# ScalarE's order in layer 0's attention: both exponentials of a tile ahead of the first copy

## The chip, the core and the metric

The kernel runs on one core of one Trainium2 chip. A core has five engines, each with its own instruction stream, that meet through semaphores: TensorE (matrix products and transposes, results into PSUM), VectorE, ScalarE, GpSimd and SyncE, which starts DMA transfers. The metric is the device time of one execution in microseconds (us), the median of the runs. A profile is one execution, in which every instruction's start and duration is recorded; its span runs from the first to the last instruction of the program.

## What is computed

A two-layer diffusion backbone over 1024 latent tokens and 256 context tokens, width 1024, all in fp32. Layer 0 mixes tokens by a pooling mixer beside differential attention; layer 1 by latent attention; each layer ends with a SwiGLU block. The change touches the differential attention of layer 0 alone:

```python
def diff_attn_core(q, k, v, lam, scale):
    s = jnp.einsum('bqhjd,bkhjd->bhjqk', q.astype(F32), k.astype(F32)) * scale
    p = jax.nn.softmax(s, axis=-1)
    pd = p[:, :, 0] - lam * p[:, :, 1]
    return jnp.einsum('bhqk,bkhe->bqhe', pd, v.astype(F32)).astype(v.dtype)
```

There are 4 heads, each with two score maps (j = 0, 1) of head width 64, and values of width 128. Latent queries see all 1280 keys; context queries see the 256 context keys. The output of each head is normalised (rmsnorm over its 128 values) afterwards.

## The kernel before

`attention0` (line 175) is one block of five engine programs. It works on N = 40 score tiles: tile n is head n // 10 and query tile q = n % 10 of 128 queries. Tiles with q < 8 are latent queries (full tiles, 1280 keys), q = 8 and 9 are context queries (256 keys). Two neighbouring tiles form a pair J (20 pairs), whose combined probabilities are transposed ("turned") in units of two key blocks: five units a pair, one for the context pair. `("u", x)` is the turn of a unit, `("v", x)` its product with the values. The order is written out by hand, in periods n:

- TensorE, in period n: the latent scores of the first map (`latent(t, 0)`, line 316; they wait for the first exponential of the tile before), then the turns of list `a`, the context scores of tile n (`context(n)`, line 306; they wait for both exponentials of tile n - 1), the latent scores of the second map (`latent(t, 1)`), then turns (line 341) and value products (line 355) of list `b` in turn, then extras.
- `work_in(n)` gives the lists. In odd n, with J = (n - 3) / 2: `a` is the turn of unit 4 of pair J - 1; `b` is value 3 of J - 1, turn 0 of J, value 4 of J - 1, turn 1 of J. In even n, with J = (n - 4) / 2: `a` is turn 2 of J; `b` is value 0, turn 3, value 1, value 2 of J. Units that a pair doesn't have drop out.
- `extras_in(n)`: in tiles 17, 27 and 37 the sums of squares of the head before (`s`, line 365, 10 products with one column), in tiles 19 to 23, 29 to 33 and 39 to 41 its factors (`b`, line 371, two transposes). They too write one of the two turn banks in PSUM.
- The turn banks: `tbank` deals them out alternately in the order of all turns and extras, and `bank_free` makes each wait until the one two back has been read: for a turn that is ScalarE's copy.
- VectorE takes the maximum over the latent scores (line 465) and context scores (line 472; 474 in context tiles), then the negated maximum of the two for each map (`negative`, line 479), the bias of the exponential. After E0 can start it computes the factor of the tile before (lines 485, 489), and then the maximum over the second map's latent scores, and that map's negated maximum. In the first tile of heads 1 to 3 both negated maxima come together, since those scores were made during the head before.
- ScalarE takes the exponentials with their row sums (`exps(n, 0)` and `exps(n, 1)`, line 413), the copies of turned units from PSUM to `pt` (`copy`, line 423), of outputs (`copy_out`, line 430), a square root for each head (line 456) and the high part of normed outputs (line 435). `exps(n, 1)` waits for `comb` (the tile two back is combined) and, in full tiles, for the second negated maximum.
- GpSimd scales the second map by its factor and adds it to the first (`combine`, lines 553, 556, 557). Turn 0 of a pair waits until both its tiles are combined.

ScalarE's loop before, lines 437 to 451 (the two statements that change places are in the middle):

```python
for n in range(PERIODS):
    a, b = work_in(n)
    ...
    if n < N:
        exps(n, 0)
    for x in turns_of(b)[:1]:
        copy(x)
    if n < N:
        exps(n, 1)
    for J in outs_of(b):
        copy_out(J)
    for x in turns_of(b)[1:]:
        copy(x)
```

The copy in the middle is that of turn 0 of a pair in odd tiles and of turn 3 in even tiles; 19 odd tiles and 15 even tiles below 40 have one.

Of the kernel before, what the change touches and what calls it, by code (L numbers as in the profile page):

```python
# [174 lines left out]
def attention0(e, qs, ks, vs, P, p1, pt, o_sb, sq, tmp, ahi, alo, pooled, mixp, w_out):  # L175
# [3 lines left out]
    N, PT, RING_P = 10 * HEADS0, 6, 6  # L179
    PAIR_COUNT, PERIODS = 5 * HEADS0, 10 * HEADS0 + 12  # L180
    first_unit = [sum(len(PAIRS0[y % 5]) for y in range(J)) for J in range(PAIR_COUNT + 1)]
    with ExitStack() as ctx:
# [10 lines left out]
        def latents_before(n):  # L193

            return 8 * (n // 10) + min(n % 10, 8)
# [17 lines left out]
        def work_in(n):  # L213

            if n % 2:
                J = (n - 3) // 2
                a = [("u", unit(J - 1, 4))]
                b = [("v", unit(J - 1, 3)), ("u", unit(J, 0)), ("v", unit(J - 1, 4)), ("u", unit(J, 1))]
            else:
                J = (n - 4) // 2  # L220
                a = [("u", unit(J, 2))] + [("v", unit(J, 0))] * (J == PAIR_COUNT - 1)
                b = [("v", unit(J, 0))] * (J < PAIR_COUNT - 1) + [("u", unit(J, 3)), ("v", unit(J, 1)), ("v", unit(J, 2))]
            return [[x for x in y if x[1] is not None] for y in (a, b)]
# [4 lines left out]
        def extras_in(n):  # L228

            return ([("s", h) for h in range(HEADS0) if SUMS_AT[h] == n]  # L230
                    + [("b", h, p) for h in range(HEADS0) for p in range(5) if SCALES_AT[h][p] == n])

        def turns_of(work):
            return [x for x in work if x[0] == "u"]

        def outs_of(work):
            return [pair_of(x[1])[0] for x in work if x[0] == "v" and x[1] + 1 == first_unit[pair_of(x[1])[0] + 1]]
# [4 lines left out]
        def last_turn(n):  # L242

            return turn_index["u", first_unit[n // 2 + 1] - 1]

        def tbank(x):
            return TB + turn_index[x] % 2 * BANK
# [4 lines left out]
        with nc.Block() as block:  # L252
            @block.sync
            def _(sp):
                def values(h):
                    if h >= 2:
                        sp.wait_ge(s["pv"], 21 * (h - 1))
                    sp.dma_start(vs[:, h % 2, :, :].rearrange("p t v -> p (t v)"), S["v0"][h, :, :]).then_inc(s[f"v{h % 2}"], 16)

                values(0)  # L260
                e.store_turn(sp, 19)
                for i in range(8, 12):
                    e.store_u(sp, i)
                for x, n in e.turns_stored:
                    sp.wait_ge(x, n)
                for h in range(1, HEADS0):
                    if h >= 2:
                        sp.wait_ge(s["ctx"], 10 * (h - 1))
                    load_keys0(e, sp, ks[h % 2], h, s[f"qk{h % 2}"])
                    load_queries0(e, sp, qs[h % 2], h, s[f"qk{h % 2}"])  # L270
                    values(h)
                for y in range(4):
                    sp.wait_ge(e.ustored[y], 48)
                sp.wait_ge(s["ctx"], N)
                u, pw, edge = pooled
                for g in range(3):
                    load_pooled(e, sp, u, g)
                    if g == 0:
                        sp.dma_start(edge[:], e.dram["pool_edge"]).then_inc(e.pool_edge, 16)
                        sp.dma_start(pw[:], e.dram["pool_w"]).then_inc(e.pool_w, 16)  # L280
                for x in range(RING):
                    load_block(e, sp, mixp, 0, x, w_out[x, :, :])
                e.clear_old(sp)

            @block.tensor
            def _(pe):
# [72 lines left out]
                def extra(x):  # L359
                    bank_free(x)  # L360
                    if x[0] == "s":
                        h = x[1]
                        pe.wait_ge(s["sq"], 5 * h + 5)
                        for q in range(10):
                            last = nc.tensor.matmul(e.ps[:, tbank(x) + q:tbank(x) + q + 1], sq[:, h % 2, q * 128:(q + 1) * 128], e.sel[:, 2:3],
                                                    start=True, stop=True)
                    else:
                        _, h, p = x
                        pe.wait_ge(s["rd"], h + 1)
                        for y, q in enumerate(tiles(h, p)):  # L370
                            last = nc.tensor.transpose(e.ps[:, tbank(x) + y * 128:tbank(x) + (y + 1) * 128],
                                                       rd[:, q:q + 1].broadcast_to([128, 128]), e.ident[:])
                    last.then_inc(s["turn"], 1)
# [21 lines left out]
            @block.scalar  # L395
            def _(act):
                def exps(n, m):
                    h, q = divmod(n, 10)
                    a = 0 if q < 8 else LAT
                    if m == 0:  # L400
                        if n >= RING_P:
                            act.wait_ge(s["turn"], last_turn(n - RING_P) + 1)
                        act.wait_ge(s["n0"], n + 1)
                        src, dst = e.ps[:, M0 + a:M0 + T], P[:, n % RING_P, a:T]
                        total = s0[:, h % 2, q:q + 1]
                    else:
                        if n >= 2:
                            act.wait_ge(s["comb"], n - 1)
                        if q < 8:
                            act.wait_ge(s["n1"], latents_before(n) + 1)  # L410
                        src, dst = e.ps[:, M1 - CTX:M1 + LAT - a], p1[n % 2][:, 0:T - a]
                        total = s1[:, n % 2:n % 2 + 1]
                    nc.scalar.activation(dst, src, ACT.Exp, bias=nb[:, n % 4, m:m + 1], accum_out=total).then_inc(s[f"e{m}"], 1)

                def copy(x):
                    u = x[1]
                    if u == 0:
                        for y in range(4):
                            act.wait_ge(e.ustored[y], 48)
                    act.wait_ge(s["turn"], turn_index[x] + 1)  # L420
                    if u >= PT:
                        act.wait_ge(s["pv"], u - PT + 1)
                    nc.scalar.activation(pt[:, u % PT, :], e.ps[:, tbank(x):tbank(x) + BANK], ACT.Copy).then_inc(s["copy"], 1)

                def copy_out(J):
                    h, p = divmod(J, 5)
                    act.wait_ge(s["pv"], first_unit[J + 1])
                    if h >= 2:
                        act.wait_ge(s["tmp"], 5 * (h - 2) + p + 1)
                    nc.scalar.activation(o_sb[:, h % 2, 256 * p:256 * p + 256], e.ps[:, OB:OB + 256], ACT.Copy).then_inc(s["out"], 1)  # L430

                def normed(h, p):
                    x = 5 * h + p
                    act.wait_ge(s["tmp"], x + 1)
                    nc.scalar.activation(ahi[:, h, 256 * p:256 * p + 256], tmp[:, x % 2, :], ACT.Copy).then_inc(s["nhi"], 1)

                for n in range(PERIODS):
                    a, b = work_in(n)
                    for x in turns_of(a):
                        copy(x)  # L440
                    for J in outs_of(a):
                        copy_out(J)
                    if n < N:
                        exps(n, 0)
                    for x in turns_of(b)[:1]:
                        copy(x)
                    if n < N:
                        exps(n, 1)
                    for J in outs_of(b):
                        copy_out(J)  # L450
                    for x in turns_of(b)[1:]:
                        copy(x)
                    for x in extras_in(n - 1):
                        if x[0] == "s":
                            act.wait_ge(s["vv"], x[1] + 1)
                            nc.scalar.activation(sd[:], vv[:], ACT.Sqrt).then_inc(s["sd"], 1)
                    for x in extras_in(n):
                        if x[0] == "b":
                            normed(*x[1:3])
# [4487 lines left out]
```

## Time and profile before

| | |
|---|---|
| time, median of 3 runs | 3234.47 us (3230.9 to 3235.47) |
| the profiled execution's span | 3233.6 us |
| TensorE busy (PE) | 3044.6 us, 94% |
| TensorE weight loads (PEld) | 2491.6 us, 77% |
| GpSimd busy (POOL) | 2288.7 us, 71% |
| VectorE busy (DVE) | 1947.3 us, 60% |
| ScalarE busy (ACT) | 1105.4 us, 34% |
| layer 0's attention | from about 302 to 549 us of the span |

Engines are named as in the profile: PE is TensorE's products, PEld its weight loads, which overlap with them, DVE VectorE, ACT ScalarE, POOL GpSimd. A row of the timeline has the start in us from the span's start, the duration in us from the first of the merged instructions to the end of the last, engine, line, operation, output<-inputs by tile names, output shape<-input shape and the number of merged instructions. In square brackets stands how long the engine had been idle before it, and who ended that; no bracket means that the engine came straight from other work. Tiles in PSUM are all called `ps`. The two buffers of the second exponential are `squares` in even tiles and `a_p` in odd ones; the first exponential always writes `a_p`.

### The profile page before, as it was taken

Reading aid. Unit: us, or ns where it says so; the run is one execution under the profiler, and the core shown is the slowest. Engines: PE = TensorE matmul, PEld = TensorE weight load, DVE = VectorE, ACT = ScalarE, POOL = GpSimd, SP = SyncE. Lnnn points to the kernel's source line nnn. Section 1 sums busy time; section 2 is a strip of 40 time slices with the busy share of each in tenths; the row PEclk is TensorE's granted clock in tenths of the full one; section 3 lists DMA queues with packets and bytes.
Section 4 is the critical chain, followed back from the end, with each engine's and each line's share of the span. In section 5 each row is a group of like instructions: output and inputs, shape, how many; then the busy total and the mean of one; then the engine's idle time right before and its main releaser. Section 6 shows DMA issues by size and latency. Waiting matters only on the chain. (4 is left out here: it accounts for less than half of the span.)

```text
span 3233.6 us, 44078 instructions
## 1 busy us (share of the span) xinstructions
PE 3044.6 (94%) x14302; PEld 2491.6 (77%) x14302; DVE 1947.3 (60%) x2544; ACT 1105.4 (34%) x1897; POOL 2288.7 (71%) x2297
## 2 busy tenths in 40 slices
PE   7998998998989999999898989999998999999999
PEld 6777876787968888888676767777776778888887
DVE  6585665777864454454535557777765765454454
ACT  4322775134620110010333446766772410010110
POOL 4584765663498888888623268888887688888885
PEclk9999998999999999999998979999999999999999
DMA  6367323457621111112203441111114211111112
GB/s 237 110 203 202 75 58 117 174 170 262 217 79 59 45 52 60 52 43 65 102 26 105 149 130 41 48 41 40 48 29 141 68 40 58 45 52 58 51 46 85
DMA packets 134922, 297.72 MB, mean 92 GB/s; under 512 B 36449, under 2 KB 69473, under 8 KB 134689
## 3 DMA queue, kind: packets, MB, share of 16 engines
q1 hardware_dynamic: 121632, 252.89, 24.8%
q10 hardware_dynamic: 13184, 43.52, 4.3%
q8 instruction: 55, 0.90, 0.1%
q14 instruction: 51, 0.41, 0.0%
HBM read 251.68 MB, written 44.63 MB: 92 GB/s over the span
## 5 line engine op out<-in xcount | busy, mean ns | idle before, releaser
L1546 POOL TENSOR_TENSOR a_pl<-a_p,a_ph 128x512 fp32r<-128x512 f32 x320 | 451.1, 1430 | 102.9 <-ACT a_p L1491 98.1
L164 PE MATMUL ps<-a_q,a_k 97*128 97x512 f32 x960 | 273.3, 398 | 1.3 <-POOL a_q L1565 1.3
L1490 ACT ACTIVATE a_ph<-ps 128x512 fp32r<-128x512 f32 x320 | 192.2, 601 | 179.4 <-PE ps L164 178.6
L1392 DVE TENSOR_REDUCE a_top<-ps 128x1 f32<-128x512 f32 x256 | 172.3, 687 | 95.4 <-PE ps L1316 95.4
L164 PE MATMUL ps<-hidden,whi 128*128 128x512 f32 x704 | 218.0, 391 | 7.2 <-POOL wlo L1849 4.3
L164 PE MATMUL ps<-mixed_hi,l_whi 128*128 128x512 f32 (+1 forms) x544 | 207.2, 381 | 10.3 <-issue 2.9
L3032 POOL TENSOR_TENSOR l_wlo<-l_raw,l_whi 128x512 fp32r<-128x512 f32 x154 | 200.4, 1301 | 12.8
L164 PEld LDWEIGHTS ps<-a_q,a_k 97*128 97x128 f32 x960 | 179.8, 191 | 38.2 <-issue 1.5
L164 PE MATMUL ps<-mixed_lo,l_whi 128*128 128x512 f32 (+1 forms) x544 | 206.4, 379 | 0.0
L164 PE MATMUL ps<-mixed_hi,l_wlo 128*128 128x512 f32 (+1 forms) x544 | 206.2, 379 | 0.0
L2485 DVE SCALAR_TENSOR_TENSOR residual<-ps,mod,residual 128x512 f32<-128x512 f32 x176 | 132.1, 750 | 109.8 <-PE ps L164 109.8
L3832 DVE SCALAR_TENSOR_TENSOR residual<-ps,mod,residual 128x512 f32<-128x512 f32 x176 | 132.0, 750 | 108.5 <-PE ps L164 108.5
L1849 POOL TENSOR_TENSOR wlo<-raw,whi 128x512 fp32r<-128x512 f32 x144 | 187.8, 1304 | 12.0
L1491 ACT ACTIVATE a_p<-ps 128x512 f32<-128x512 f32 x320 | 192.7, 602 | 0.0
L3236 PE MATMUL ps<-l_factor,l_whi 128*128 128x512 f32 x528 | 164.1, 392 | 7.2 <-POOL l_wlo L3032 7.2
L164 PEld LDWEIGHTS ps<-hidden,whi 128*128 128x128 f32 x704 | 132.7, 189 | 35.7 <-issue 8.0
L1584 PE MATMUL ps<-mixed_hi,l_whi 128*128 128x256 f32 (+1 forms) x472 | 147.8, 313 | 10.8 <-POOL mixed_lo L3106 3.3
L2054 PE MATMUL ps<-l_factor,whi 128*128 128x512 f32 x480 | 147.9, 389 | 0.0
L1584 PE MATMUL ps<-mixed_lo,l_whi 128*128 128x256 f32 (+1 forms) x472 | 146.6, 311 | 0.0
L1584 PE MATMUL ps<-mixed_hi,l_wlo 128*128 128x256 f32 (+1 forms) x472 | 146.3, 310 | 0.0
L3236 PE MATMUL ps<-mixed_hi,l_whi 128*128 128x512 f32 x352 | 138.0, 392 | 4.6 <-POOL l_wlo L3032 3.8
L164 PE MATMUL ps<-hidden,wlo 128*128 128x512 f32 x352 | 137.7, 391 | 0.0
(421 smaller groups left out, 8886.3 us busy)
## 6 DMA issues: line engine op xcount, KB each, us to landing
l_raw<-in_w_ffn SPq DMA_DIRECT2D x132, 512.0 KB, 3.9
raw<-in_w_ffn SPq DMA_DIRECT2D x66, 512.0 KB, 3.6
l_row<-in_mod_t ACTq DMA_DIRECT2D x32, 512.0 KB, 4.5
f_vraw<-in_mod_t ACTq DMA_DIRECT2D x24, 512.0 KB, 4.1
a_k<-scratch_k SPq DMA_DIRECT2D x32, 320.0 KB, 6.8
f_raw<-in_w_in SPq DMA_DIRECT2D x16, 512.0 KB, 5.4
l_raw<-in_w_out SPq DMA_DIRECT2D x16, 512.0 KB, 5.2
l_shared_row<-in_mod_t ACTq DMA_DIRECT2D x16, 512.0 KB, 6.3
```

The source lines that it names most:

```text
L164: last = nc.tensor.matmul(out, a, b, start=at == 0, stop=at == n - 1)
L1392: nc.vector.tensor_reduce(top[:, q:q + 1, c], e.ps[:, bank:bank + BANK], AX.X, ALU.max).then_inc(s["auxr"], 1)
L1490: nc.scalar.activation(ph[:, kk % 2, c], b, ACT.Exp).then_inc(s["exp"], 1)
L1491: nc.scalar.activation(p[:, kk % 2, c], b, ACT.Exp).then_inc(s["exp"], 1)
L1546: nc.gpsimd.tensor_tensor(pl[:, kk % 2, c], p[:, kk % 2, c], ph[:, kk % 2, c].bitcast(F32), ALU.subtract).then_inc(s["pl"], 1)
L1584: last = nc.tensor.matmul(out, a, b, start=k == 0 and x == 0, stop=k == n - 1 and x == 2)
L1849: nc.gpsimd.tensor_tensor(wl[:, slot(pos), :], of, wh[:, slot(pos), :].bitcast(F32), ALU.subtract).then_inc(s["half"], 1)
L2054: last = nc.tensor.matmul(e.ps[:, bank:bank + BANK], a[:, slot(pos), w], b, start=k == 0 and x == 0, stop=k == 3 and x == 2)
L2485: last = nc.vector.scalar_tensor_tensor(h[:, m, a:a + w], e.ps[:, o:o + w], e.mod[:, g, c:c + 1], h[:, m, a:a + w], ALU.mult, ALU.add)
L3032: nc.gpsimd.tensor_tensor(wl[:, slot(pos), :], of, wh[:, slot(pos), :].bitcast(F32), ALU.subtract).then_inc(s["half"], 1)
L3236: last = nc.tensor.matmul(e.ps[:, at:at + BANK], a[:, slot(pos), w], b, start=k == 0 and x == 0, stop=k == 3 and x == 2)
L3832: nc.vector.scalar_tensor_tensor(h[:, m, a:a + w], e.ps[:, o:o + w], e.mod[:, 40 + m, 0:1], h[:, m, a:a + w], ALU.mult, ALU.add).then_inc( ...
```

## The change

In every period in which a tile is scored, ScalarE now takes both exponentials in a row, and the copy of the first turned unit of list `b` comes behind them. The copies of list `a` stay ahead of the first exponential, the output copy and the remaining copies stay behind, and no other engine's program changes. No instruction, wait or buffer is added or removed.

```diff
@@ -442,10 +442,9 @@
                         copy_out(J)
                     if n < N:
                         exps(n, 0)
+                        exps(n, 1)
                     for x in turns_of(b)[:1]:
                         copy(x)
-                    if n < N:
-                        exps(n, 1)
                     for J in outs_of(b):
                         copy_out(J)
                     for x in turns_of(b)[1:]:
```

## Rows read from the trace of the kernel before

**Rows 1.** The page: busy us, share of the span, instructions, for each engine

```profile
PE 3044.6 (94%) x14302; PEld 2491.6 (77%) x14302; DVE 1947.3 (60%) x2544; ACT 1105.4 (34%) x1897; POOL 2288.7 (71%) x2297
```

**Rows 2.** Busy table: length, busy PE, PEld, DVE, ACT, POOL, granted clock, DMA, GB/s

```profile
302.50:537.50 235.00, 213.83 (x1178) 176.76 (x1178) 143.06 (x291) 158.79 (x288) 161.80 (x126) 0.96 0.33 86
...
458.50:462.00 3.50, 3.50 (x15) 3.10 (x15) 2.02 (x4) 0.60 (x1) 0.72 (x2) 0.59 0.00 0
```

**Rows 3.** Waits, 302 to 538 us: us in total, times, longest

```profile
ACT a_p L413 <- DVE a_negmax L479: 43.8, 33, 5.7
...
PEld ps L306 <- issue: 11.1, 13, 1.4
```

**Rows 4.** Timeline, tile 25 and the head of tile 26

```profile
443.17 1.33 ACT L413 ACTIVATE a_p<-ps,a_negmax 128x1280 f32<-128x1280 f32 x1 [1.14 <-DVE a_negmax L479]
...
444.49 0.59 ACT L423 ACTIVATE a_pt<-ps 128x512 f32<-128x512 f32 x1
...
444.67 0.15 DVE L479 TENSOR_REDUCE a_negmax<-a_max 128x1 f32<-128x2 f32 x1
...
444.97 1.33 ACT L413 ACTIVATE a_p<-ps,a_negmax 128x1280 f32<-128x1280 f32 x1
...
445.15 1.17 PE L316 MATMUL ps<-a_k,a_q 128*128 128x512 f32 x4
...
446.16 0.60 PE L341 MATMUL ps<-ident,a_p 128*128 128x128 f32 x4
...
446.27 0.40 ACT L430 ACTIVATE a_o<-ps 128x256 f32<-128x256 f32 x1
...
446.54 0.71 PE L306 MATMUL ps<-a_k,a_q 128*128 128x256 f32 x4
...
447.50 0.68 DVE L472 TENSOR_REDUCE a_max<-ps 128x2 f32<-128x512 f32 x1
```

**Rows 5.** Timeline, tile 12, which has no copy between its exponentials

```profile
370.27 1.33 ACT L413 ACTIVATE a_p<-ps,a_negmax 128x1280 f32<-128x1280 f32 x1 [1.66 <-DVE a_negmax L479]
...
372.01 1.33 ACT L413 ACTIVATE squares<-ps,a_negmax 128x1280 f32<-128x1280 f32 x1 [0.33 <-DVE a_negmax L479]
```

**Rows 6.** Timeline, tile 13's first exponential and tile 14's context scores

```profile
375.38 1.33 ACT L413 ACTIVATE a_p<-ps,a_negmax 128x1280 f32<-128x1280 f32 x1 [1.67 <-DVE a_negmax L479]
...
378.74 0.71 PE L306 MATMUL ps<-a_k,a_q 128*128 128x256 f32 x4 [0.26 <-ACT a_p L413]
```

**Rows 7.** Timeline, tile 17: first exponential and the sums of squares

```profile
397.71 1.33 ACT L413 ACTIVATE a_p<-ps,a_negmax 128x1280 f32<-128x1280 f32 x1 [1.14 <-DVE a_negmax L479]
...
399.77 2.29 PE L365 MATMUL ps<-sel,a_sq 128*128 128x1 f32 x20
```

**Rows 8.** Timeline, tile 23 and the head of tile 24

```profile
431.19 1.33 ACT L413 ACTIVATE a_p<-ps,a_negmax 128x1280 f32<-128x1280 f32 x1 [1.36 <-DVE a_negmax L479]
...
432.51 0.59 ACT L423 ACTIVATE a_pt<-ps 128x512 f32<-128x512 f32 x1
...
433.15 0.43 PE L371 MATMUL ps<-ident,a_rstd 128*128 128x128 f32 x2 [0.95 <-ACT a_pt L423]
...
433.34 1.17 PE L316 MATMUL ps<-a_k,a_q 128*128 128x512 f32 x4
...
434.95 0.66 PE L341 MATMUL ps<-ident,a_p 128*128 128x128 f32 x4 [0.44 <-ACT a_pt L423]
...
435.36 0.61 PE L306 MATMUL ps<-a_k,a_q 128*128 128x256 f32 x3
```

**Rows 9.** Timeline, tile 20's first exponential and tile 21's first turn

```profile
415.56 1.33 ACT L413 ACTIVATE a_p<-ps,a_negmax 128x1280 f32<-128x1280 f32 x1 [0.93 <-DVE a_negmax L479]
...
418.49 0.60 PE L341 MATMUL ps<-ident,a_p 128*128 128x128 f32 x4
```

**Rows 10.** Timeline, tile 11's context scores

```profile
363.29 0.53 PEld L306 LDWEIGHTS ps<-a_k,a_q 128*128 128x128 f32 x4 [0.28 <-issue]
```

**Rows 11.** Timeline, tile 9's first turn in list b

```profile
356.00 0.42 PEld L341 LDWEIGHTS ps<-ident,a_p 128*128 128x128 f32 x4 [0.66 <-POOL a_p L557]
```

## Prediction

> **What bounds the kernel now.** I read the page first: TensorE is busy 94% [rows 1] of a span of 3233.6 us, and the weight products of the later stages, which the change doesn't touch, follow in the same order. So the question is what happens to the end of layer 0's attention. The busy table of that stage [rows 2] covers 235.0 us: TensorE is busy 213.8 of them, ScalarE 158.8, GpSimd 161.8, VectorE 143.1. The reader is to see two things there: ScalarE has a third of its time free, so its total work sets nothing, and TensorE has only 21 us free. The table of waits of the stage [rows 3] says for whom ScalarE waits: 43.8 us in 33 waits for VectorE's negated maximum (line 479), the bias of an exponential. Last, the timeline of one full tile, number 25 [rows 4], for the order and the distances.
>
> In tile 25 the first exponential (below: E0) starts at 443.17, the copy of the first turned block at 444.49, the second exponential (E1) at 444.97. VectorE finishes the second map's negated maximum at 444.67 + 0.15 = 444.82, so E1 starts only 0.15 after its bias is there, 1.80 after E0. Meanwhile TensorE goes from the next tile's scores (445.15) to the turn (446.16) and the context scores (446.54) without an idle stretch. That turn writes the PSUM bank that the copy of 444.49 empties: there are two banks, and bank_free makes each turn wait for the copy two turns back.
>
> **What moves.** No instruction is added or removed. 34 tiles have such a copy (19 odd, 15 even); each now stands behind E1.
>
> *What E1 gains.* Next to nothing in a full tile: where no copy stands between, tile 12, E0 starts at 370.27 and E1 at 372.01, 1.74 later, after a wait of 0.33 for line 479 [rows 5]. With the copy it is 1.80. The other bound is 1.32 (444.49 - 443.17), the distance to an instruction that waits for nothing, a gain of 0.48. I take 0.06: in tile 25 the maximum is ready 1.65 after E0, which fits a start at 1.74.
>
> *What the copy loses.* E1 now starts at E0 + 1.74; what follows E1 without a wait starts 1.30 behind it (444.97 to 446.27), so the copy starts at E0 + 3.04 instead of E0 + 1.32 and ends, 0.59 long, at E0 + 3.63: 1.72 later. Whether that costs anything is decided by who wants the bank, tile by tile. A turn that waited starts 0.06 after the copy's end (I take this from tile 23, where the factor's 433.15 follows a copy of 0.59 that began 1.32 behind E0, at 432.51), and the context scores follow 0.41 behind it (434.95 to 435.36) [rows 8]; queued it is 0.38 (446.16 to 446.54). So a waiting turn comes at E0 + 3.69, the context scores at E0 + 4.10.
>
> 1. Tiles 5, 15, 25, 35: the turn at the head of the next tile wants the bank. Tile 25: context scores at 443.17 + 4.10 = 447.27 instead of 446.54: +0.73, on an engine with no idle stretch here. 4 x 0.73 = 2.9.
> 2. Tiles 3 and 13: same turn. TensorE waited for E1 anyway, context scores at 378.74 [rows 6]; they come at 375.38 + 4.10 = 379.48: +0.74. 1.5.
> 3. Tile 7: the same 0.73, but in tile 9 TensorE stands 0.66 for GpSimd [rows 11], whose chain follows the context maximum. In the like tile VectorE starts that maximum at 447.50, 0.25 after the context scores' end (446.54 + 0.71) [rows 4], and absorbs as much. +0.5.
> 4. Tiles 17, 27, 37: the sums of squares (line 365) take the bank at the end of the same tile, ahead of the next scores. Tile 17: 397.71 + 3.69 = 401.40 instead of 399.77 [rows 7]: 1.63, and VectorE and GpSimd hang behind it alike. 3 x 1.6 = 4.8.
> 5. Tiles 23 and 33: the factor (line 371) takes it. It waited already, at 433.15; now 431.19 + 3.69 = 434.88, +1.73, and the scores behind it 433.34 + 1.73 = 435.07. The turn after them had waited until 434.95 and now comes 1.01 behind the scores (445.15 to 446.16), 436.08, the context scores at 436.46 instead of 435.36 [rows 8]: +1.1. 2.2.
> 6. Tiles 20 and 30, even, with a factor in them: the turn at the head of the next tile wants the bank. In the first tile of a head VectorE makes both negated maxima together, so E1 can start at E0 + 1.32, the copy at + 2.62, its end at + 3.21: 415.56 + 3.27 = 418.83 instead of 418.49 [rows 9], 0.3, and 0.4 at the context scores. 0.8.
> 7. Tile 10, the same without a factor: the bank isn't wanted, E1 comes up to 0.48 sooner, and TensorE stood 0.28 for it [rows 10]: -0.3.
> 8. The other even full tiles (4, 6, 14, 16, 24, 26, 34, 36): the bank and the late block are wanted only in the second half of the next tile: 0. Tiles 11, 21, 31: no turn follows; E1's 0.06 each, -0.2. The eight context tiles (exponentials of 256 columns): the first copy there waits for TensorE, not for its place; their E1 comes sooner, which can help by 0 to 0.48 at the three boundaries where a square root follows. Nearest is tile 9, where TensorE waits for GpSimd [rows 11], so -0.1 each, -0.3.
>
> Sum: 2.9 + 1.5 + 0.5 + 4.8 + 2.2 + 0.8 - 0.3 - 0.2 - 0.3 = **+11.9 us**. The cover of the even tiles in group 8 is the distance between a turn and its product; were it gone, each would cost some 0.73 as in group 1, 5.8 for the eight. Behind the stage everything starts later by the same amount; its first weight blocks are asked for when the last context scores are done, and shift along.
>
> One rule bears on a term. ScalarE frees itself 1.32 after an exponential's start by the row. The Trainium skill (ScalarE: Activation LUTs, What ACT_TABLE_LOAD costs) says that activations back to back overlap by about 93 ns; by it the distance would be 1.24, and the sum some 1 us smaller. The row decides.
>
> **Rivals.** *A: TensorE steps around the wait.* The scores behind a waiting factor have their own semaphore met; if TensorE ran them ahead, the stalls would shrink to almost nothing: 3234.5. Against it: at 433.15 the factor waited for a copy though the scores behind it had been free since E0's end at 431.19 + 1.33 = 432.52, and they started at 433.34, behind it [rows 8]. The Trainium skill (TensorE: Matmul & The Clock Gate, Architectural detail) gives TensorE's queue a partial reorder window that pulls weight loads ahead of matmuls in flight; of going past a wait it claims nothing. 0.06.
>
> *B: faster.* If the second maximum were ready at E0 + 1.32, E1 would come 0.48 sooner, and the context scores, ahead of which the weight loads stand idle 13 times (11.1 us, line 306; the table says issue, the product side names ScalarE [rows 3, 6]), with it: 13 x 0.48 = 6.2, and with 0.3 for the square roots 6.5, provided no bank is wanted: 3228. It decides from the point where line 479 ends before the copy starts; in tile 25 it ended 0.33 after that, and the 33 waits speak against it. 0.03.
>
> *C: the clock falls more.* From 458.5 to 462.0, right behind the sums of squares of the second head, the granted clock was 0.59 [rows 2], between the levels 2.4 and 1.2 GHz: (1 - 0.59) x 3.5 = 1.4 us of work pushed back. New stalls stand just ahead of the three blocks of sums. Three more such stretches give +4.2: 3250.6. If the stretches of before vanish, about -2.8. The Trainium skill (same page, Part 1) has the gate throttled by default and released by activity, which agrees in direction; the rows don't show where the point lies. 0.13.
>
> *D: something else holds those turns anyway* (GpSimd's combined tile): 3234.5. Against it, the timeline names the copy in tile 23, and in tile 25 nothing. 0.04.
>
> **Numbers.** The forecast, 0.74: the profiled run's span 3233.6 + 11.9 = 3245.5; the median of the runs is 0.9 above that span, so 3246.4. Ends: releases 0.2 cheaper in 11 places and stretches of low clock that vanish give -5; rival C gives +4.2, and the runs of before spread from 3230.9 to 3235.5, so I add 2. Range 3240.5 to 3252.5, which leaves out A, B and D (0.13) and some of C. 0.2% is about 6.5 us, what a measurement of this kernel can tell from no change. Faster 0.03; same A, D and the forecast halved: 0.12; slower 0.85.
>
> **What would show it.** In the changed profile: E1 1.74 behind E0 in full tiles, the copy 3.04 behind E0; idle time of TensorE on line 341 for ScalarE's copy up to about 7 us, on line 365 three new waits of 1.6; the context scores of tiles 24 and 34 late by 1.1; ScalarE's busy time unchanged; the stage longer by about 12 and nothing behind it longer. Wrong if line 306 rather than 341 carries the new idle time, if E1 comes at 1.32, or if a copy's delay is felt in the even tiles of group 8.

## The result and the profile after

The changed kernel takes 3254.44 us (median of 4 runs, 3249.99 to 3258.06) against 3233.08 us for the kernel before, measured beside it: a ratio of 1.0058, interval 1.0043 to 1.0072. A second measurement, below, gave 1.0063 (1.0049 to 1.0078). By these ratios it is slower by 19 to 20 us (by the two differences of medians 21 and 23), where 12 were forecast; the median lies 1.9 us above the upper end of the range.

The page of the changed kernel; the profiled execution is the slowest of the four:

```profile
span 3256.3 us, 44078 instructions
...
PE 3057.2 (94%) x14302; PEld 2501.1 (77%) x14302; DVE 1950.5 (60%) x2544; ACT 1109.8 (34%) x1897; POOL 2287.6 (70%) x2297
```

ScalarE's busy time is nearly that of before, 1109.8 us for 1105.4. The busy table cuts the run at the context scores of tile 3, those of tile 39 (the "stage" from here on) and the last factor. Before first; the columns are those of [rows 2]:

```profile
321.85:522.78 200.93, 188.44 (x1069) 158.50 (x1069) 127.00 (x259) 141.00 (x255) 147.88 (x113) 0.98 0.23 55
522.78:546.18 23.40, 16.75 (x101) 13.35 (x100) 8.05 (x20) 11.95 (x27) 12.61 (x19) 0.89 0.47 166
546.18:3233.60 2687.42, 2556.56 (x11848) 2084.95 (x11848) 1610.18 (x1974) 847.92 (x1445) 1944.52 (x2053) 0.98 0.26 83
```

The changed kernel, cut at the same places:

```profile
320.14:542.02 221.88, 197.69 (x1068) 165.03 (x1069) 128.74 (x259) 145.35 (x255) 147.80 (x113) 0.95 0.21 50
542.02:565.38 23.36, 16.89 (x101) 13.42 (x99) 8.12 (x20) 11.71 (x27) 12.74 (x19) 0.89 0.47 166
565.38:3256.30 2690.92, 2562.28 (x11848) 2089.53 (x11848) 1611.50 (x1974) 848.14 (x1445) 1943.20 (x2053) 0.97 0.26 83
```

The stage is 221.88 us instead of 200.93, +20.95; the end of the attention is as long as it was; the 2690 us behind it are 3.5 us longer. In the 13 other profiles of this document, of kernels that are all alike there, that last stretch lay between 3.2 us shorter and 5.4 us longer than in the first profile of before: it is no effect of the change, but it hides small ones in the time.

Two things stand in the stage. The first is the waits. Tile 25 and the head of tile 26, as in [rows 4]; line numbers behind the edit are one lower than before:

```profile
451.28 1.33 ACT L413 ACTIVATE a_p<-ps,a_negmax 128x1280 f32<-128x1280 f32 x1 [1.14 <-DVE a_negmax L478]
...
452.78 0.15 DVE L478 TENSOR_REDUCE a_negmax<-a_max 128x1 f32<-128x2 f32 x1
...
453.02 1.33 ACT L413 ACTIVATE a_p<-ps,a_negmax 128x1280 f32<-128x1280 f32 x1 [0.32 <-DVE a_negmax L478]
...
454.34 0.59 ACT L423 ACTIVATE a_pt<-ps 128x512 f32<-128x512 f32 x1
...
454.98 0.66 PE L341 MATMUL ps<-ident,a_p 128*128 128x128 f32 x4 [0.54 <-ACT a_pt L423]
...
455.40 0.72 PE L306 MATMUL ps<-a_k,a_q 128*128 128x256 f32 x4
...
456.15 0.69 DVE L471 TENSOR_REDUCE a_max<-ps 128x2 f32<-128x512 f32 x1 [0.45 <-PE ps L306]
```

E1 stands 1.74 behind E0 after a wait of 0.32 for VectorE's negated maximum, as tile 12 did before [rows 5]; the copy starts 3.06 behind E0 instead of 1.32; TensorE's turn waits 0.54 for it (its weight load 0.98), and VectorE, which had come straight from its latent maximum, now waits 0.45 for the context scores. Tile 17 [rows 7]:

```profile
399.53 1.33 ACT L413 ACTIVATE a_p<-ps,a_negmax 128x1280 f32<-128x1280 f32 x1 [1.15 <-DVE a_negmax L478]
...
402.58 0.59 ACT L423 ACTIVATE a_pt<-ps 128x512 f32<-128x512 f32 x1
...
403.23 2.39 PE L365 MATMUL ps<-sel,a_sq 128*128 128x1 f32 x20 [1.47 <-ACT a_pt L423]
```

The sums start 3.70 behind E0, where 3.69 was forecast, after 1.47 of idle time. At the factor of tile 23 TensorE already stood 0.95 before [rows 8]; now it stands 2.69:

```profile
440.32 0.43 PE L371 MATMUL ps<-ident,a_rstd 128*128 128x128 f32 x2 [2.69 <-ACT a_pt L423]
```

The waits of the stage with the changed order ([rows 3] is the same view of before):

```profile
ACT a_p L413 <- DVE a_negmax L478: 47.3, 48, 5.9
...
PEld ps L341 <- ACT a_pt L423: 10.8, 12, 1.5
...
PEld ps L306 <- issue: 10.4, 10, 1.6
...
PEld ps L371 <- ACT a_pt L423: 9.5, 5, 2.9
...
PEld ps L365 <- ACT a_pt L423: 5.1, 3, 1.7
```

Before, line 341's loads stood 4.8 us for the copy, line 371's 4.4, line 365's nothing. ScalarE's waits for the maximum went from 33 to 48: some of them had been hidden by the copy that stood in front.

The second thing is TensorE's clock. Five stretches of the changed kernel; their granted clock is the third number from the end:

```profile
406.50:410.00 3.50, 3.50 (x14) 3.11 (x13) 2.26 (x4) 1.42 (x5) 0.44 (x1) 0.51 0.00 0
440.60:444.20 3.60, 3.60 (x15) 3.10 (x14) 1.75 (x3) 1.17 (x3) 1.79 (x3) 0.53 0.00 0
467.90:474.90 7.00, 7.00 (x28) 6.31 (x28) 2.40 (x6) 0.68 (x2) 0.18 (x1) 0.51 0.00 0
505.50:509.00 3.50, 3.39 (x12) 2.89 (x13) 1.44 (x2) 1.07 (x4) 2.17 (x3) 0.51 0.00 0
532.80:539.70 6.90, 6.90 (x30) 6.43 (x31) 1.71 (x6) 1.70 (x6) 1.23 (x2) 0.51 0.02 4
```

Before had only the like of the third and the last, and those half as long:

```profile
459.10:462.50 3.40, 3.40 (x13) 2.90 (x12) 2.15 (x4) 0.60 (x1) 0.12 (x1) 0.50 0.00 0
517.10:520.60 3.50, 3.50 (x16) 3.02 (x14) 1.94 (x6) 1.16 (x3) 1.31 (x2) 0.51 0.03 7
```

All are at 1.2 GHz. By the clock records of the trace the stage spends 23.9 us at that level, before 6.8. The first, third and last begin within 4 us of the start of the sums of squares of tiles 17, 27 and 37, the other two at the factors of tiles 23 and 33.

### The profile page after: what moved, and what is told of

The parts are those of the page before. It is cut to its first block and busy times, and to the rows that moved or that the text cites. A ratio compares the mean times of both kernels' runs of the same rounds, so it can differ in the third digit from the quotient of the medians.

```text
span 3256.3 us, 44078 instructions
## 1 busy us (share of the span) xinstructions
PE 3057.2 (94%) x14302; PEld 2501.1 (77%) x14302; DVE 1950.5 (60%) x2544; ACT 1109.8 (34%) x1897; POOL 2287.6 (70%) x2297
```

## The experiments

Each compares its stage, from the context scores of tile 3 to those of tile 39, with 197.64 us, the length that the kernel before has with no half-clock time in it (experiment 7). "Waits" is the time by which the stage grows through later context scores alone, tile by tile. Where the clock was low in a tile, the step is taken from a run that had the full clock there (4, 8 and 9); those of 3, 5 and 6 are in part estimates of this kind.

The recorded expectations reckon with 12.7 us for the changed kernel. It is 13.1: they count each block of sums with the 1.64 by which it starts later, but the context scores behind it come 1.73 to 1.74 later at full clock, since a block that had to wait takes 2.39 us instead of 2.30. "Theory 1" in them is the reading just given: only a turn, factor or block of sums that wants the bank of the late copy stalls TensorE, and the long ones of these stalls bring the clock down too.

| kernel | stage | waits | at half clock | time, ratio to before |
|---|---|---|---|---|
| before, first and second profile | 200.93, 200.91 | 0 | 6.8, 6.8 | 1 |
| changed | 221.88 | 13.1 | 23.9 | 1.0058 (1.0043 to 1.0072) |
| changed, again | 223.39 | 13.1 | 27.3 | 1.0063 (1.0049 to 1.0078) |
| 1 even tiles alone | 202.94 | 0.5 | 10.2 | 0.9994 (0.9985 to 1.0004) |
| 2 turn tiles alone | 204.56 | 5.3 | 3.4 | 1.0004 (0.9995 to 1.0014) |
| 3 sum and factor tiles alone | 214.32 | 7.4 | 20.5 | 1.0056 (1.0040 to 1.0073) |
| 4 changed, stalls filled | 215.46 | 13.1 | 10.2 | 1.0042 (1.0028 to 1.0055) |
| 5 before, TensorE waits longer | 217.36 | 8.5 | 23.9 | 1.0058 (1.0038 to 1.0078) |
| 6 changed, sums and factors later | 215.40 | 11.4 | 13.7 | 1.0056 (1.0037 to 1.0074) |
| 7 before, wide sums | 197.64 | 0 | 0 | 0.9986 (0.9975 to 0.9997) |
| 8 changed, wide sums | 215.50 | 13.1 | 10.2 | 1.0039 (1.0024 to 1.0054) |
| 9 changed, filled and wide | 212.32 | 13.1 | 3.4 | 1.0031 (1.0020 to 1.0042) |
| 10 wide sums, both in a row in tile 10 and context tiles | 197.51 | 0 | 0 | 0.9986 (0.9975 to 0.9997) |

In every row with low clock the stage is 197.6, plus the waits, plus 0.45 to 0.48 us for each us at half clock: some 1.6 us for a stretch of 3.4.

**Which copies cost: 1 to 3.** The changed order in some tiles alone; `both` is the one thing that differs:

```diff
+                    both = n % 2 == 0                        # 1, even_tiles
+                    both = n in (3, 5, 7, 13, 15, 25, 35)    # 2, turn_tiles
+                    both = n in (17, 23, 27, 33, 37)         # 3, extra_tiles
                     if n < N:
                         exps(n, 0)
+                    if n < N and both:
+                        exps(n, 1)
                     for x in turns_of(b)[:1]:
                         copy(x)
-                    if n < N:
+                    if n < N and not both:
                         exps(n, 1)
```

> Both exponentials in a row in the even tiles alone (15 of the 34 moved copies). Theory 1 (only a turn or factor that wants the bank of the late copy stalls TensorE): stalls of 0.3 to 0.4 in tiles 20 and 30, tile 10 gains 0.3, nothing elsewhere; the context scores of tile 39, counted from those of tile 3, are at most 0.5 us later than before, and the time is that of before within 1 us. Theory 2 (every moved copy costs alike, 20.9 us of the stage over 34 copies = 0.6 each): 15 x 0.6 = 9 us later.

> Both in a row only in tiles 3, 5, 7, 13, 15, 25 and 35, where a turn at the head of the next tile wants the bank. Theory 1: 0.75 each, 0.5 in tile 7: the stage is 5.0 us longer, and no new stretch of low clock appears in it, since the stalls are short: time 5 us above before. If short stalls bring the clock down too: new half-clock stretches behind these tiles, 1.7 us each, and 7 us or more.

> Both in a row only in tiles 17, 23, 27, 33 and 37, where the sums of squares or a factor want the bank. The waits alone: 3 x 1.64 + 2 x 1.1 = 7.1 us. Theory 1 (the long stalls ahead of these also bring the clock down, as in the changed kernel's trace at 406, 440, 468, 505 and 533 us): 7 + about 8 = 15 us, with five or so low stretches. Rival (the low stretches come from where the clock's phase happens to lie, not from these stalls): 7 us, and low stretches as in before.

The waits came as theory 1 had them. Even tiles: 0.32 in tiles 20 and 30, -0.31 in tile 10, nothing in the eight of group 8; theory 2 falls. The stage was nevertheless 2.0 us longer, because the clock fell once more than before, behind the sums of tile 17, where nothing had been made to wait (busy table of even tiles alone):

```profile
401.00:404.60 3.60, 3.60 (x15) 3.17 (x14) 2.41 (x5) 1.62 (x5) 0.69 (x1) 0.53 0.00 0
```

Turn tiles: 0.80, 0.77, 0.75, -0.21 (given back in front of tile 10), and 0.75 four times, and less half-clock time than before rather than more: the clock fell behind the sums of tile 27 alone. Its time, 1.3 us above before (-1.6 to 4.5), doesn't resolve the 3.6 us of its stage. Sum and factor tiles: the sums 1.64 later three times, the context scores behind the factors 1.1 twice, and 20.5 us at half clock, in these stretches of the busy table of that kernel:

```profile
402.40:406.00 3.60, 3.60 (x14) 3.10 (x13) 2.26 (x4) 1.16 (x3) 0.22 (x1) 0.53 0.00 0
436.50:440.20 3.70, 3.70 (x15) 3.17 (x14) 2.05 (x3) 1.07 (x3) 1.67 (x3) 0.54 0.00 0
463.80:467.40 3.60, 3.60 (x15) 3.11 (x16) 1.19 (x3) 0.00 (x0) 0.00 (x0) 0.53 0.00 0
498.00:504.90 6.90, 6.14 (x20) 5.17 (x21) 3.23 (x7) 3.16 (x7) 3.33 (x4) 0.51 0.01 2
528.80:532.30 3.50, 3.50 (x14) 2.94 (x13) 1.37 (x4) 1.41 (x4) 1.61 (x2) 0.52 0.01 2
```

By the stage these five tiles of 34 bring 13.4 of the 20.95 us: 7.4 of waits and the rest clock. By the time (1.0056) it looks like the whole loss, but the interval reaches down to 1.0040, and the profiled execution, 3243.4 us, is the fastest of four that otherwise took 3254 to 3256.

**Does the order matter, or the stall: 5.** ScalarE's order is that of before:

```diff
+                    if n in (17, 23, 27, 33, 37):
+                        pe.wait_ge(s["copy"], work_in(n)[1][-1][1] + 1)
                     for x in extras_in(n):
                         extra(x)
```

> The kernel before, ScalarE's order untouched; in tiles 17, 23, 27, 33 and 37 TensorE waits, ahead of the sums of squares or the factor, until the copy of turn 1 is done too (it ends at 401.69 in tile 17 of before, 434.90 in tile 23). Theory 1 (a stall of TensorE there costs its length and brings low clock, whoever makes it): 3 x 1.98 at the sums and 2 x 1.2 at the context scores behind the factor, 8.3 us of waits, and about 6 of clock: 14 us, as the kernel with both exponentials in a row in these tiles. Rival (the order on ScalarE itself costs something, as later maxima or factors): 8 us at most and the clock as before.

The sums came 1.97 later three times and the clock spent 23.9 us at half. The stage is 16.4 us longer than before, 8.5 of waits and 8 of clock, more than the 14 expected and less than the changed kernel's 20.95, which has the waits of the turn tiles too; the ratio 1.0058 (1.0038 to 1.0078) doesn't resolve that difference. Its timeline at tile 17, the last exponential and the block of sums:

```profile
398.00 1.33 ACT L415 ACTIVATE a_p<-ps,a_negmax 128x1280 f32<-128x1280 f32 x1
...
400.23 2.39 PE L365 MATMUL ps<-sel,a_sq 128*128 128x1 f32 x20 [1.80 <-ACT a_pt L425]
```

So a stall of TensorE there has this price, with ScalarE's order as before: the stall costs, and not the order itself.

**Filling the stall: 4.** Real products in it, the order and every wait of the changed kernel kept:

```diff
+                    if n in (17, 23, 27, 33):
+                        if n % 10 == 7:
+                            arrived((n + 3) // 10)
+                        latent(scores_in(n + 1), 0, True)    # no semaphore; overwritten
                     for x in extras_in(n):
                         extra(x)
```

> The changed kernel, and in tiles 17, 23, 27 and 33 TensorE makes the first map's scores of the next tile once more, ahead of the sums of squares or the factor: 1.2 us of real products that lie inside the stall of 1.6 or 1.7 and are overwritten. Nothing is left out. Theory 1: the waits stay what they are, the low stretches at 406, 440, 468 and 505 go, that at 533 (tile 37, not filled) stays: 12 + 2 = 14 us above before, 6 to 7 below the changed kernel. Rival (low stretches by phase alone): as the changed kernel, 21 us above before, or more by the work added.

The timeline of tile 17, products of the filling and the sums behind them:

```profile
401.65 0.85 PE L316 MATMUL ps<-a_k,a_q 128*128 128x512 f32 x3
...
403.04 2.39 PE L366 MATMUL ps<-sel,a_sq 128*128 128x1 f32 x20 [0.54 <-ACT a_pt L428]
```

And of tile 23, the filling and the factor:

```profile
437.89 1.20 PE L316 MATMUL ps<-a_k,a_q 128*128 128x512 f32 x4 [0.45 <-ACT a_p L418]
...
440.12 0.43 PE L372 MATMUL ps<-ident,a_rstd 128*128 128x128 f32 x2 [1.03 <-ACT a_pt L428]
```

The sums still wait for the copy (0.54, the rest is now work) and come 1.64 late; the factor's 2.69 of idle time is now 0.45, products, and 1.03. At the two factors the low stretches are gone: the context scores of tiles 24 and 34 come 1.09 and 1.10 later, the forecast's 1.1, where the changed kernel had 2.1 and 2.4. Behind the sums of tiles 17 and 27 they stayed, against the expectation. The one of tile 27 is half as long, but so is that of tile 37, which was not filled, so that this can't be put down to the filling. A stall of 0.54 is left there; that a fall needs none is shown by before and by the even tiles alone.

**The sums themselves: 7 and 8.**

```diff
-    nc.tensor.matmul(e.ps[:, tbank(x) + q:tbank(x) + q + 1], sq[...], e.sel[:, 2:3], ...)
+    nc.tensor.matmul(e.ps[:, tbank(x) + 48 * q:tbank(x) + 48 * q + 48], sq[...], e.sel[:, 2:50], ...)
```

VectorE's read of the sums is changed with it, to take the first of each 48.

> The kernel before; the sums of squares are made with 48 columns of ones instead of one (all 48 results alike, VectorE reads the first), so that TensorE streams columns while it loads the squares as weights. Theory 1's second half says that the low clock behind tiles 27 and 37 of before (459 and 517 us) comes from the block of one-column products itself: no stretch of low clock between 310 and 540 us, the block's own length unchanged (0.115 a product), the stage 3 us shorter, time 0.1% lower. Rival (the stretches are chance): low stretches as before, or the block longer.

> The changed kernel with the same 48 columns in the sums. Waits as in the changed kernel, 12.7 us. Theory 1: the low stretches behind the sums (406, 468 and 533 us there, 17 us at half clock together) go or shorten, those at the factors (440, 505) stay, 6.8 us: stage 12.7 + 0.46 x 0 to 7 us, 13 to 16 us longer than before. If the stalls ahead of the sums bring the clock down and not the sums: as the changed kernel, 20 us.

In the kernel before, no half-clock time is left in the stage, and the block is as long as with one column (2.33 us; 2.29 in tile 17 of before [rows 7]). A block of sums in the timeline of that kernel:

```profile
454.81 2.33 PE L365 MATMUL ps<-sel,a_sq 128*128 128x48 f32 x20
```

The stage in its busy table:

```profile
320.30:517.94 197.64, 185.38 (x1068) 155.84 (x1069) 127.00 (x259) 140.94 (x255) 146.62 (x113) 1.00 0.23 56
```

The stage is 3.3 us shorter and the time 0.14% lower (0.03 to 0.25). With the changed order the stretches behind tiles 17 and 37 went; one behind tile 27 stayed, 6.8 us long, and one at the factor of tile 33. That at the factor of tile 23 went too, against the expectation and though TensorE stood 2.69 there as before. Where a stall of 1.5 stands ahead, wide sums don't always help. Which of the two decides in a given place stays open.

**Both remedies: 9.**

> The changed kernel with both remedies: the next scores made once more inside the stalls of tiles 17, 23, 27 and 33, and 48 columns in the sums of squares. It separates waits from clock. Theory 1: every wait as in the changed kernel, the granted clock 1.00 or one stretch at most (tile 37), so that the stage (context scores of tile 3 to those of tile 39) is 197.6, as before with wide sums, + 12.7 = 210.3 us. If the waits had been sized wrongly and the clock counted for less, the length stays near 215.

The stage in the busy table of this kernel:

```profile
320.46:532.78 212.32, 192.77 (x1085) 159.38 (x1085) 126.78 (x259) 145.22 (x255) 146.89 (x113) 0.99 0.22 53
```

212.3 with one stretch of 3.4 us left, in tile 37, which was not filled: 197.6 + 13.1 + 1.6. The expectation, 210.3 and one stretch at most, was short by 0.4 in the waits. With the clock nearly taken out, the waits are 1.2 above the forecast's 11.9.

**If TensorE went around the wait: 6.** The extras of tile n stand behind `latent(t, 0)` of period n + 1.

> The changed kernel with TensorE's sums of squares and factors issued behind the next tile's first scores instead of ahead of them (the order of the turn banks stays). What rival A asked of the hardware is here done by the program. Theory 1: in tiles 17 and 27 1.2 of the 1.64 us is covered by those scores, in 23 and 33 0.65 of the 1.1; 3.7 us less waiting, the 0.75 of tiles 3 to 35 stays: about 9 us of waits in the stage instead of 12.7. If VectorE, which takes the sums ahead of its next maximum, hands the delay on instead, the context scores of tile 19 come as late as in the changed kernel.

Half a success. In tiles 17 and 27 the next scores covered 0.9 of the 1.73 by which the context scores come later, in 23 and 33 some 0.3 of the 1.1, and the context scores of tiles 22 and 23 (32 and 33) together lost 0.4 more than with the changed order; the factors come 0.9 to 2.4 later there. Waits 11.4 instead of 13.1, where 9 was expected. That VectorE, which takes sums and factors in its own order, hands the rest on fits this and is not shown by a run of its own. The time doesn't show the shorter stage: 1.0056 (1.0037 to 1.0074), and the profiled execution is the fastest of its four.

**Better than both: 10.** Wide sums, and `both = n % 10 >= 8 or n == 10`.

> Towards a version better than both: the kernel before with wide sums, and both exponentials in a row only where the changed trace showed a gain or nothing (tile 10 and the context tiles, q = 8 and 9). Theory 1: tile 10 gives 0.3, the others 0 to 0.1 each: the stage 0.3 to 0.7 us shorter than with wide sums alone, the time 0.1 to 0.2% below before. If the order cost something by itself: longer than with wide sums alone.

Tile 11's context scores come 0.31 sooner, and tile 12's have lost 0.23 of it again. The stage is 0.13 us shorter than with wide sums alone, where 0.3 to 0.7 was expected; the ratio is the same 0.9986. The gain is that of the wide sums.

**Repeats.**

> The kernel before once more, unchanged, for a second profile of it. If the low stretches behind the sums of squares depend on where the execution stands when it reaches them, their number between 310 and 540 us differs from the two of the first profile (0 to 3), and the stage is 197.6 us + some 1.6 for each; the order of events and all waits are the same to 0.05 us. If they are fixed: two again, 200.9 us.

> The changed kernel once more, unchanged, for a second profile and a narrower interval. Theory 1: the waits of the stage as in the first profile to 0.05 us (0.75, 1.64 and so on, 12.7 in all); the low stretches behind the three blocks of sums and the two factors are there again, 17 to 24 us at half clock, since each has its cause in the program, so that the stage is 218 to 222 us and the time 17 to 21 us above before. If the stretches of the first profile were an accident of that execution: 3 to 7 us at half clock, stage 212 to 214, time 10 to 13 above before.

Before: the same two stretches, the stage the same to 0.02 us; the rival "where the execution stands" falls for these two profiles, which doesn't make the number fixed: the turn tiles alone had one such stretch and the even tiles alone three, with nothing waiting ahead of any block of sums. Changed: every wait again within 0.03, and 27.3 us at half clock instead of 23.9 (the one behind tile 17 was twice as long), which is outside what was expected, on the far side. How long a stretch gets does vary: the eight of 6.8 us at sums all began 0.7 to 1.7 us after the block's first product, inside the block, those of 3.4 us 1.8 us or more after it.

**All 14 profiles together.** Whether the clock fell, at the three blocks of sums (tiles 17, 27, 37) and the two factors (23, 33):

| place | TensorE idle just ahead | runs | falls |
|---|---|---|---|
| sums, one column | none | before twice, 1, 2 | 8 of 12 |
| sums, one column | 0.5 to 0.6 us | 4, 6 (17 and 27) | 4 of 4 |
| sums, one column | 1.5 to 1.8 us | changed twice, 3, 5; 4, 6 (37) | 14 of 14 |
| sums, 48 columns | none | 7, 10 | 0 of 6 |
| sums, 48 columns | 0.6 us | 9 (17 and 27) | 0 of 2 |
| sums, 48 columns | 1.5 us | 8; 9 (37) | 2 of 4 |
| factor | 0.9 to 1.0 us | before twice, 1, 2, 7, 10 | 0 of 12 |
| factor | 1.0 us | 4, 6, 9 | 1 of 6 |
| factor | 2.7 us | changed twice, 3, 5, 8 | 9 of 10 |

A stall makes a fall much likelier in both places, and one-column sums bring falls by themselves. What settles a single place is not shown.

## Why the forecast fell short

**The exponentials' distance: right.** 1.74 from tile 6 on in all full tiles but the first of a head, 1.32 there; tiles 2 to 5 kept 1.80. The reason named, that E1 waits for the maximum in VectorE's order, is what the new wait of 0.32 in tile 25 shows.

**The groups: right, to 0.3 us each, for groups 1 to 6.** Turn at the head of the next tile: 0.75 (0.73 forecast), 0.78 (0.74) for tiles 3 and 13, 0.53 for tile 7 (0.5), the missing part absorbed in front of tile 10 as argued. Sums: 1.64 later (1.6), the context scores behind them 1.73, a step that the forecast took to be the same. Factors of tiles 23 and 33: 1.09 at full clock (1.1). Tiles 20 and 30: 0.32 (0.4). The eight even tiles of group 8: 0. All waits together 13.1; 11.9 forecast.

**Group 7 and the small gains of group 8: wrong in size.** Tile 10's 0.31 was there, but tile 11's first exponential hangs on VectorE, which takes the latent scores first and so had no use for context scores that came sooner; 0.17 was given back a tile later. Nothing was gained at the square roots. Some 0.6 us too hopeful.

**The clock: the step that failed.** The sum has no term for it. It stood beside the sum, as rival C, with a chance of 0.13 and 1.4 us for each of three more stretches. Three more came, behind the sums of tile 17 and at both factors, and the two of before were twice as long: 17.1 us more at half clock, which cost the stage 7.9 us (20.95 - 13.1), not 4.2. The forecast's waits alone would have been 1.2 us short. The row that could have warned was one of [rows 2]: in the kernel before the clock fell behind the second block of sums with TensorE busy throughout, in an execution with no stall ahead of it, so that stalls put exactly there should have been taken as likely to bring more, not as a rare chance. The two factors, which already stood 0.95 for a copy [rows 8], were not thought of in rival C. The Trainium skill (TensorE: Matmul & The Clock Gate, Part 1) had the direction, throttled by default and released by activity. The falls behind long stalls agree with it; those in the kernel before came with TensorE recorded as busy throughout. The runs give the price in this kernel, 0.45 to 0.48 us for each us at half clock.

**The range.** Its lower end doesn't follow from its terms: 3246.4 less 5 is 3241.4, and 3240.5 is 5 below 3245.5, the figure without the 0.9. Nothing hangs on it here.

**Rivals A, B and D: fallen.** TensorE let the free scores stand behind the waiting factor and the sums (6 shows what letting them pass would give); line 306 stood 10.4 us, for 11.1 before, instead of gaining 6; and the turns waited for ScalarE's copy, which the timeline names.

## What to carry to other kernels

An engine that works in order is delayed by what its slowest consumer frees last: before moving a step on a lightly loaded engine, list for each buffer who waits for it next and how many instructions stand behind that wait. Here 29 of 34 moved copies cost 5.6 us of waits together, and five cost 7.4 us and, with the clock, about two thirds of the loss of the stage. And where TensorE runs small products or stands just ahead of them, a stall has a second price in clock; a few more columns can cost nothing and take that price away, where the weight loads set the pace (2.31 of the 2.39 us of the block of sums in experiment 4).

## What the runs showed of the hardware

- Products of one column and of 48 columns, with 128 x 128 weights each in fp32, take the same 2.3 us for 20; with 48 and no stall ahead the clock stayed at 2.4 GHz at all six blocks of two kernels, with one it fell behind two of three (before, two profiles), three (even tiles alone) or one (turn tiles alone).
- Those falls came with TensorE recorded as busy the whole time (3.50 of 3.50 us in [rows 2]): the busy share doesn't tell that the clock will hold.
- At the factors, two transposes, the clock never fell when TensorE had stood 0.95 us ahead of them (12 places) and fell in 9 of 10 when it had stood 2.7.
- A us at 1.2 GHz instead of 2.4 cost this stage 0.45 to 0.48 us.
